# Two-layer encoder with a sorted mixture of experts: rows gathered four blocks ahead, expert matrices in two transfers each

## The reference

```python
def _hier_moe(h, w_group, b_group, w_expert, b_expert, w1, w3, w2):
    pg = jax.nn.softmax((xt @ w_group).astype(jnp.float32) + b_group.astype(jnp.float32), axis=-1)
    g_val, g_idx = lax.top_k(pg, 1)
    ...
    e_val, e_idx = lax.top_k(pe, MOE_TOPK)
    gate = g_val[:, None] * e_val / jnp.sum(e_val, axis=-1, keepdims=True)
    ...
    def expert_block(args):
        xblk, e = args
        return (jax.nn.silu(xblk @ w1[e]) * (xblk @ w3[e])) @ w2[e]

def reference(x, ...):
    for l in range(DEPTH):
        h = _rmsnorm(x, norm_mix[l])
        if l % 2 == 0:
            x = x + _even_mixer(h, ...)
        else:
            x = x + _diff_attention(h, ...)
        h = _rmsnorm(x, norm_ffn[l])
        x = x + _hier_moe(h, ...)
    return _rmsnorm(x, norm_final)
```

## Time and profile before

| | |
|---|---|
| median of 3 runs | 1602.75 us (1597.41 to 1604.11) |
| profiled execution | 1602.87 us, of which the span is 1601.0 us |
| mean granted TensorE clock | 0.931 |
| PE busy, share of the span | 1305.1 us (82%) |
| DVE | 931.1 us (58%) |
| ACT | 504.7 us (32%) |
| POOL | 351.2 us (22%) |
| moved by DMA | 455.63 MB, mean 285 GB/s |
| in 188 transfers of 2048 KB | w1 and w3: 124, median 29.8 us to landing; w2: 64, median 33.2 us |

### The profile page before, as it was taken

How to read it: one execution, slowest core, us unless ns; L and a number is a source line. 1 busy time by engine, 2 the same in 40 slices (tenths; PEclk the granted TensorE clock), 3 DMA queues, 4 the chain that set the end, 5 groups by cost and what they waited for, 6 DMA issues and landing times.

```text
span 1601.0 us, 40258 instructions
## 1 busy us (share of the span) xinstructions
PE 1305.1 (82%) x16222; PEld 850.9 (53%) x16223; DVE 931.1 (58%) x1888; ACT 504.7 (32%) x927; POOL 351.2 (22%) x443
## 2 busy tenths in 40 slices
PE   7998995887887787686999899958858987579884
PEld 5874684554454444355888445845425544346553
DVE  4476635676564556377232896356636765437676
ACT  4416733222221222123223586222212222112222
POOL 4020002333232333132000001023313332213332
PEclk9999996999998899797999999969979999889997
DMA  4313047999999999992232112689999499997972
GB/s 168 106 55 138 2 184 296 406 429 425 429 427 427 428 429 427 428 390 81 102 105 82 49 46 76 252 307 403 429 427 427 168 428 428 425 429 317 426 289 93
DMA packets 60222, 455.63 MB, mean 285 GB/s; under 512 B 6100, under 2 KB 7696, under 8 KB 26816
## 3 DMA queue, kind: packets, MB, share of 16 engines
q1 hardware_dynamic: 53712, 439.01, 66.8%
q0 software_dynamic: 4656, 8.41, 1.4%
q10 hardware_dynamic: 1728, 6.29, 1.0%
HBM read 451.68 MB, written 6.32 MB: 286 GB/s over the span
## 4 chain that ended last, share of the span: by engine, by line
PE 51%; DMA 33%; DVE 7%; issue 5%; ACT 2%; POOL 1%; POOLq 0%; DVEq 0%; SPq 0%; ACTq 0%
DMA wu<-in_w 21%; PE bank L396 18%; DMA xg<-hn_dram,icol 12%; PE bank L856 12%; PE bank L873 4%; PE bank L826 2%; PE bank L816 2%; PE bank L630 2%; PE bank L719 1%; PE bank L731 1%; PE bank L684 1%; DVE hh L1535 1%; PE bank L695 1%; ACT sgate L1123 1%; PE bank L574 1%
## 5 line engine op out<-in xcount | busy, mean ns | idle before, releaser
L856 PE MATMUL bank<-wu,xT 128*32 128x256 f32 x6080 | 388.4, 412 | 137.7 <-DMA wu<-in_w 74.8
L1529 DVE TENSOR_TENSOR X<-bank,X 128x512 f32<-128x512 f32 x776 | 481.0, 682 | 7.5 <-PE bank L826 4.5
L856 PEld LDWEIGHTS bank<-wu,xT 128*32 128x32 f32 x6080 | 212.1, 118 | 286.8 <-issue 192.5
L873 PE MATMUL bank<-wd,hT 128*32 128x256 f32 x3040 | 185.7, 384 | 5.3
L1535 DVE TENSOR_TENSOR hh<-bank,sgate 64x256 f32<-64x256 f32 x95 | 40.4, 426 | 244.2 <-ACT sgate L1123 244.2
L1644 POOL TENSOR_SCALAR Sm<-CT,tgc 128x512 fp32r<-128x512 f32 x95 | 149.4, 1572 | 53.8 <-PE bank L826 53.8
L363 DVE TENSOR_TENSOR wlo<-raw,whi 128x512 fp32r<-128x512 f32 (+1 forms) x112 | 77.1, 699 | 137.5 <-ACT whi L355 137.4
L1123 ACT ACTIVATE sgate<-bank 64x256 f32<-64x256 f32 x95 | 35.8, 377 | 370.9 <-PE bank L856 370.9
L1628 POOL COPY icol<-idxI 128x1 uint32 (+1 forms) x97 | 17.9, 184 | 578.9 <-PE bank L816 552.0
L1130 ACT ACTIVATE yhi<-bank,tgc 128x256 fp32r<-128x256 f32 x95 | 45.0, 474 | 289.1 <-PE bank L826 289.1
L873 PEld LDWEIGHTS bank<-wd,hT 128*32 128x32 f32 x3040 | 101.4, 110 | 63.6 <-issue 25.0
(11 more groups left out here) (227 smaller groups left out, 1656.2 us busy)
## 6 DMA issues: line engine op xcount, KB each, us to landing
wu<-in_w SPq DMA_DIRECT2D x124, 2048.0 KB, 29.8
wd<-in_w SPq DMA_DIRECT2D x64, 2048.0 KB, 33.2
raw<-in_od_w_in SPq DMA_DIRECT2D x12, 1024.0 KB, 5.2
wu<-in_w SPq DMA_DIRECT2D x8, 1024.0 KB, 15.5
raw<-in_ev_w_in SPq DMA_DIRECT2D x6, 1024.0 KB, 5.3
raw<-in_ev_w_out SPq DMA_DIRECT2D x4, 1024.0 KB, 8.1
hn_dram<-HN ACTq DMA_DIRECT2D x8, 512.0 KB, 5.8
raw<-in_od_w_out SPq DMA_DIRECT2D x4, 1024.0 KB, 9.9
```

The costliest lines, as they stand in the source:

```text
L856: last = pe.matmul(B[1][q * SLOT:q * SLOT + SLOT, 0:HH], xT[:, k, :], WU[slot_of(e, q // 2)][:, k, q % 2 * HH:q % 2 * HH + HH], start=k == ...
L873: last = pe.matmul(B[3][q * SLOT:q * SLOT + SLOT, 0:DQ], hT[:, k, :], WD[slot_of(e, 2)][:, k, q * DQ:q * DQ + DQ], start=k == 0, stop=k == ...
L1529: dve.tensor_tensor(xq, B[4 + q][:, :].rearrange("p (t c) -> p t c", t=2), xq, ALU.add).then_inc(signal, 1)
```

## The change

- **Rows.** `xg` has two buffers, for even and odd blocks, each with a semaphore of its own. ACT copies the rows of a block from `xg` to a new tile `xs` at the end of its pass, behind `yhi`, and PE transposes `xs`. The gather of block b+4 follows the selection of block b on POOL, whose loop runs over pairs of blocks. PE does one of the two row transposes ahead of the transposes of `hh` and one behind them. The index tables have NBLK + 4 columns. `Sm` moves to another place in memory.
- **Weights.** Each w1 and w3 comes by two transfers, each of four of the eight k-slices, which are 8 KB per partition; PE's counts are 32, 32 and 16 for the three pieces.
- **End of an expert stage.** The first half of the last token sums goes into banks 0 to 3, the second into banks 4 to 7. PE first waits for the last gathers.
- **Start of layer 0 and of layer 1.** ACT and DVE split the first weight slice of layer 0 ahead of the activations; in both layers the first dense matmuls wait for one `lo` slice at a time.
- **Attention of layer 0.** The exponentials at L1000 move behind the softmax exponentials of the step n = 1, and DVE's multiplies to n = 4 to 7.
- DVE loads `tot` ahead of its wait for `s_vidx`. Several semaphores are put together.

```diff
-        xg = mw.take("xg", [P, DQ])
+        xg = mw.take("xg", [P, 2, DQ])
+        xs = mw.take("xs", [P, DQ])
         xT = mw.take("xT", [P, KD, SLOT])
         hh = mw.take("hh", [2 * SLOT, HH])
         sgate = mw.take("sgate", [P, HH])
         yhi, ylo = mw.take("yhi", [P, DQ], F32R), mw.take("ylo", [P, DQ], F32R)
-        Sm = mw.take("Sm", [P, T], F32R)
-        hT = Region(tail_at + 9 * KB, tail_size - 9 * KB).take("hT", [P, FK, SLOT])
+        tl = Region(tail_at + 8 * KB, tail_size - 8 * KB)
+        Sm = tl.take("Sm", [P, T], F32R)
+        hT = tl.take("hT", [P, FK, SLOT])
...
-                if chunk:
+                if chunk and (k or not first):
                     pe.wait_ge(chunk, base + max(k + 1, first))
                 for a in range(n_banks):
+                    if chunk and first and k == 0:
+                        pe.wait_ge(chunk, base + a + 1)
...
                 if j < 2:
-                    sp.dma_start(WU[k][:, :, :], (w1, w3)[j][l, src].rearrange("e (p k) f -> p (e k) f", p=P)).then_inc(s_piece[k], 16)
+                    for half in range(2):
+                        ks = slice(half * KD // 2, (half + 1) * KD // 2)
+                        sp.dma_start(WU[k][:, ks, :], (w1, w3)[j][l, src].rearrange("e (p k) f -> p (e k) f", p=P)[:, ks, :]).then_inc(s_piece[k], 16)
...
-                def row_transposes():
-
-                    for a in range(2):
-                        last = pe.transpose(B[0][:, a * P:a * P + P], xg[:, a * P:a * P + P], ident)
+                def row_transposes(parts):
+
+                    for a in parts:
+                        last = pe.transpose(B[0][:, a * P:a * P + P], xs[:, a * P:a * P + P], ident)
                     return last
...
+                        token_sums(1)
+                        pe.wait_ge(s_xcp[l], b + 4)
+                        row_transposes((0,))
                         pe.wait_ge(s_tabs, l + 1)
                         pe.wait_ge(s_h[l], b + 1)
                         for a in range(2):
                             last = pe.transpose(B[2][:, 2 * a * SLOT:2 * (a + 1) * SLOT], hh[:, a * P:a * P + P], ident[0:2 * SLOT, 0:2 * SLOT])
                         last.then_inc(s_htr[l], 1)
-                        pe.wait_ge(s_xg[l], 16 * b + 32)
-                        row_transposes().then_inc(s_xtr[l], 1)
+                        row_transposes((1,)).then_inc(s_xtr[l], 1)
...
-                pe.wait_ge(s_xg[l], 16)
-                row_transposes().then_inc(s_xtr[l], 1)
+                pe.wait_ge(s_xcp[l], 3)
+                row_transposes((0, 1)).then_inc(s_xtr[l], 1)
...
-                token_sums(0, {0: (s_add[l], 8 * tot + 1)})
-                token_sums(1, {q: (s_mo[l], q + 1) for q in range(NQ)})
+                pe.wait_ge(s_xT[l], tot + 1)
+                pe.wait_ge(s_xcp[l], tot + 4)
+                for odd in range(2):
+                    pe.wait_ge(s_xg[odd][l], 16 * (tot >> 1) + 32)
+                token_sums(0, bank=0)
+                token_sums(1, bank=0)
+                token_sums(2, {0: (s_add[l], 8 * tot + 1)})
+                token_sums(3)
...
+                splits(0, ks=(0,))
                 mixer_input(0, 0, hi0, range(4))
-                for k in range(4):
+                for k in range(1, 4):
                     splits(0, ks=(k,))
-                    mixer_input(0, 0, hi0, (k + 4,))
+                    mixer_input(0, 0, hi0, (k + 3,))
+                mixer_input(0, 0, hi0, (7,))
...
-                for c in range(4):
-                    act.wait_ge(s_grs, c + 1)
-                    act.activation(hpad[:, c, 0:T], hpad[:, c, 0:T], ACT.Exp, scale=-0.5).then_inc(s_gnr, 1)
...
+                    if n == 1:
+                        for c in range(4):
+                            act.wait_ge(s_grs, c + 1)
+                            act.activation(hpad[:, c, 0:T], hpad[:, c, 0:T], ACT.Exp, scale=-0.5).then_inc(s_gnr, 1)
...
+                for b in range(2):
+                    act.wait_ge(s_xg[b][l], 16)
+                    if b:
+                        act.wait_ge(s_xtr[l], b)
+                    act.activation(xs[:, :], xg[:, b, :], ACT.Copy).then_inc(s_xcp[l], 1)
...
+                    act.wait_ge(s_xg[0][l], 16 * ((b + 2) >> 1) + 16)
+                    act.wait_ge(s_xg[1][l], 16 * ((b + 3) >> 1))
+                    act.wait_ge(s_xtr[l], b + 2)
+                    act.activation(xs[:, :], xg[:, bass.ds(act.snap(b & 1), 1), :].rearrange("p o c -> p (o c)"), ACT.Copy).then_inc(s_xcp[l], 1)
...
-                    if 2 <= n < 6:
-                        c = n - 2
+                    if 4 <= n < 8:
+                        c = n - 4
...
-                add_sums(0, s_mo[l])
+                add_sums(0, s_mo[l], bank=0)
...
-                def gather(b):
+                def gather(b, odd):
 
                     nxt = b + 1 if isinstance(b, int) else pool.snap(b + 1)
-                    pool.wait_ge(s_xtr[l], nxt)
-                    pool.tensor_copy(icol[:, :], idxI[:, b:b + 1] if isinstance(b, int) else idxI[:, bass.ds(b, 1)]).then_inc(s_icol[l], 1)
+                    pool.wait_ge(s_xcp[l], nxt)
+                    pool.tensor_copy(icol[:, odd:odd + 1], idxI[:, b:b + 1] if isinstance(b, int) else idxI[:, bass.ds(b, 1)]).then_inc(s_icol[l], 1)
                     pool.wait_ge(s_hnst, 16 * TT * (l + 1))
                     pool.wait_ge(s_icol[l], nxt)
-                    pool.indirect_dma_start(out=xg[:, :], out_offset=None, in_=hn_dram[l].rearrange("t (q c) -> (t q) c", q=NQ),
-                                            in_offset=bass.IndirectOffsetOnAxis(ap=icol[:, :], axis=0),
-                                            bounds_check=last_row, oob_is_err=False).then_inc(s_xg[l], 16)
+                    pool.indirect_dma_start(out=xg[:, odd, :], out_offset=None, in_=hn_dram[l].rearrange("t (q c) -> (t q) c", q=NQ),
+                                            in_offset=bass.IndirectOffsetOnAxis(ap=icol[:, odd:odd + 1], axis=0),
...
-                gather(0)
-                pool.wait_ge(s_bktfin, 32)
-                pool.tensor_scalar(Sm[:, :], iotaT, neghalf[:, 0:1], None, ALU.is_equal).then_inc(s_sel1[l], 1)
-                gather(1)
+                gather(0, 0)
+                gather(1, 1)
                 pool.wait_ge(s_bktfin, 32)
                 pool.wait_ge(s_gate, 2 * l + 2)
-                with pool.Fori(0, pool.snap(tot - 1)) as b:
-                    gather(pool.snap(b + 2))
-                    selection(b)
-                selection(pool.snap(tot - 1))
+                pool.tensor_scalar(Sm[:, :], iotaT, neghalf[:, 0:1], None, ALU.is_equal).then_inc(s_sel1[l], 1)
+                gather(2, 0)
+                gather(3, 1)
+                pairs = pool.snap(tot >> 1)
+                with pool.Fori(0, pairs) as i:
+                    for odd in range(2):
+                        selection(pool.snap(2 * i + odd))
+                        gather(pool.snap(2 * i + odd + 4), odd)
+                selection(pool.snap(2 * pairs))
```

More of the change, by code:

```diff
@@ L800, in router @@
                     for q in range(NQ):
-                        last = pe.matmul(B[5][q * SLOT:q * SLOT + SLOT, 0:NBLK + 1], slotsel[:, j, :], blkt[:, j, :], start=j == 0, stop=j == 7)
+                        last = pe.matmul(B[5][q * SLOT:q * SLOT + SLOT, 0:NBLK + 4], slotsel[:, j, :], blkt[:, j, :], start=j == 0, stop=j == 7)
                 last.then_inc(s_idx, 1)
@@ L806, in router @@
                     for q in range(NQ):
-                        last = pe.matmul(B[6][q * SLOT:q * SLOT + SLOT, 0:NBLK + 1], slotsel[:, j, :], blkv[:, j, :], start=j == 0, stop=j == 7)
+                        last = pe.matmul(B[6][q * SLOT:q * SLOT + SLOT, 0:NBLK + 4], slotsel[:, j, :], blkv[:, j, :], start=j == 0, stop=j == 7)
                 last.then_inc(s_vidx, 1)
@@ L811, in experts, with token_sums @@
                 pe.wait_ge(s_tabs, l + 1)
-                def row_transposes():
-                    for a in range(2):
-                        last = pe.transpose(B[0][:, a * P:a * P + P], xg[:, a * P:a * P + P], ident)
-                    return last
-                def token_sums(half, waits):
-                    for t in (2 * half, 2 * half + 1):
-                        for part in (yhi, ylo):
-                            for q in range(NQ):
-                                if t % 2 == 0 and part is yhi and q in waits:
-                                    pe.wait_ge(*waits[q])
-                                last = pe.matmul(B[4 + q][:, t % 2 * DQ:t % 2 * DQ + DQ], Sm[q * SLOT:q * SLOT + SLOT, t * P:t * P + P],
-                                                 part[q * SLOT:q * SLOT + SLOT, :], start=part is yhi, stop=part is ylo)
-                    last.then_inc((s_sum, s_sumd)[half][l], 1)
+                def row_transposes(parts):
+                    for a in parts:
+                        last = pe.transpose(B[0][:, a * P:a * P + P], xs[:, a * P:a * P + P], ident)
```

(12 more changed lines are left out.)

115 lines of the change are left out of this document (60 added, 55 removed).

## The result

The changed kernel takes 1587.6 us in the median (1587.14 to 1589.31, 6 runs) beside 1603.05 us of the kernel before in the same runs: a ratio of 0.9906, 95% interval 0.9885 to 0.9926, some 15 us less. Its profiled execution has a span of 1586.8 us (1601.0 before).

A forecast was written before the change was run, and what follows sets the result against it. The weight stream binds three expert stretches, PE two, plus all work ahead of the first experts. From 1602.87 us, -4.8 -1.8 -2.1 -2.2 -2.0 +0.3 = -12.6 gives 1590.3; range 1579 to 1603.

The forecast's parts named there:

- Gather: Expert blocks: gathering four ahead removes PE's waits, gain 4.8 us (4 to 5.7); the other 13 of 18.8 change nothing.
- the bytes are the same: Weight stream: halved w1 and w3 move the same bytes in 124 more transfers, 8 KB runs costing 0 +-0.1 us.
- Halves: Weight stream: two transfers for each w1 and w3 cost 0, between -4 and +18 us (88 x 0.2).
- The rival of an issue's price for each transfer: Weight stream: each of 88 halved matrices pays 0.43 us, 38 in all, giving 1628; chance 0.09.
- the estimate by the fixed cost a transfer: Weight stream: 2 us more for every halved matrix, 176 us for 88, giving 1766; no row shows it.
- Start of layer 0: First dense matmul of layer 0 starts near 15.4 instead of 17.26 us: gain 1.8, between 0 and 3.6.
- more than summed: Rival: shorter PE idle time spares slow-clock time in three places; with a late raw end some 8 us more, 1582; chance 0.11.
- Exponentials: Attention of layer 0: four moved exponentials (2.19 us) fit into a later wait; gain 2.1, between 1 and 2.2.
- Between the layers: End of layer 0: adds back to back, gain 2.2; start of layer 1: dense matmuls released sooner, gain 2.0.
- End of layer 1: Last token sums: PE's wait for the last gather costs 1.7, banks return 1.4 at most: +0.3, between -1 and +1.
- ACT: Each block: row copy costs 0 within 1.85 us of room; rival: 1 us over costs 32, giving 1622, chance 0.05.
- The rival that the early gains do not carry: Whole kernel: early gains are lost in the stream or blocks, leaving about 6 us of gain, 1597; chance 0.20.

The follow-up runs named there:

- a_whole: The changed kernel with w1 and w3 loaded by one transfer each again: 1586.88 us, ratio 0.9903.
- a_best: The changed kernel with whole w1 and w3 transfers and PE's wait for the last gathers behind the first half of the last token sums: 1584.69 us, ratio 0.9885.
- b_early: The kernel before with only the edits outside the blocks; one xg buffer, gathers and weight transfers as before: 1586.61 us, ratio 0.9906.
- b_pstride: The kernel before with w1 and w3 by two transfers each, of even and odd partitions, in 16 KB runs: 1606.1 us, one execution.
- b_split: The kernel before with only the two transfers for each w1 and w3, in 8 KB runs: 1602.62 us, ratio 0.9995.
- a_slack1: The changed kernel with one more ACT copy of 1024 columns in each block, ahead of the gate's table load: span 1589.1 us.
- a_slack2: The changed kernel with two more ACT copies of 1024 columns in each block, ahead of the gate's table load: span 1594.1 us.
- b_phalf: The kernel before with w1 and w3 by two transfers each, of the lower and upper 64 partitions, in 16 KB runs: 2338.2 us, one execution.

## Why the prediction was right, step by step

The time lay 3 us under the forecast of 1590.3, in its range and on its side. Of the steps some were too small, and two parts that I had treated as independent were not. That the total came out so near is in part luck: clock that I had not counted gave some 3 us, and the stream that I had put at nothing took 2.6.

*Gather.* The waits were worth what the PE-bound stretches showed, 4.3 us for the 4.8 taken (a_whole and a_best against before, b_early and b_pstride). That 13 of the 18.8 us would change nothing held too, to about 1 us: the changed kernel was 5.2 us ahead at block 0, 10.2 at block 19, and 4.2 at block 38, behind the full queue, and with whole transfers the gather edit takes the stream from 682.4 to 683.7 us (before, b_early, b_pstride) to 681.4 and 681.7 (a_whole, a_best). The over 12 us from landing to use that I had expected were not there: behind the first four blocks the copy comes some 14 us or more behind the issue, and behind the landing, where the trace has it, 7.4 us at the least. That was room enough. What failed is the step "the bytes are the same" for the halves: it asked what shorter runs do to the piece and not what they do to the other queue that shares the DMA engines. They bring the gather forward, so the halves alone take 3.4 us of the 4.3, and the gather edit beside them 0.9.

*Halves.* Taken as 0 between -4 and +18; the stream pays 2.6 us, 0.03 us for each of 88 matrices. Landings read to 0.1 us, on which the 0 rested, could not show that. The rival of an issue's price for each transfer (38 us) fell with b_split, and so did the estimate by the fixed cost a transfer of the Trainium skill, DMA: Bandwidth & Descriptors, section "Anatomy of one DMA" (176 us): behind a full queue it isn't paid, b_pstride shows no cost beyond some 1 us for twice the transfers. That section fits its 2 us to transfers issued by GpSimd; the weights here are issued by SyncE. Nor did the rule of at least 1 MiB a DMA (the Trainium skill, the same page, section "Rules for kernel authors") speak against this edit, as I had written: the halves have 1 MiB each.

*Start of layer 0.* The first dense matmul starts at 15.49 where 15.4 was expected, 1.8 us earlier:

```profile
15.49 0.47 PE L400 MATMUL bank<-whi,hi 128*128 128x512 f32 x1 [1.31 <-DVE lo L1198]
```

But PE then also ran at full clock, which I had left to the rival "more than summed". The windows of the first 4.5 us of matmuls, before and after:

```profile
17.20:21.70 4.50, 4.44 (x12) 3.49 (x13) 4.45 (x8) 2.69 (x5) 0.00 (x0) 0.62 0.01 5
```

```profile
15.40:20.00 4.60, 4.50 (x20) 3.73 (x21) 4.60 (x8) 4.60 (x10) 0.00 (x0) 1.00 0.29 113
```

Twelve matmuls against twenty: 1.6 us more, 3.4 in all for the 1.8 taken. This one is no chance of one execution: all five kernels here without the edit stood idle for 3.52 us at this place and then ran at 0.50 to 0.62, all nine with it at 1.00 after 0.7 to 1.9 us.

*Exponentials.* The third exponential starts at 140.11 without a wait, 145.90 before:

```profile
140.11 0.69 ACT L1023 ACTIVATE P<-bank,nmx 128x512 f32<-128x512 f32 x1
```

PE's matmuls behind the attention are 4.95 us ahead, those before that place 3.4: 1.6 us for the 2.1 taken.

*Between the layers.* The adds behave as forecast, twelve of them in 7.3 us with no idle time:

```profile
L1558 DVE TENSOR_TENSOR X<-bank,X 128x512 f32<-128x512 f32 x12 | 7.3, 677 | 0.0
```

The sum of 4.2 was too small: kernels with these edits take 341.1 to 342.4 us between the layers, those without 345.5 to 349.0, 6.0 us between the means. From block 44 to the first dense matmul the edit gives 4.5 us of them (29.2 to 24.7 in the mean), near the sum. The rest, 1.5, lies behind that matmul and is the clock again; of the kernels without the edit the 345.5 is b_split, whose dense matmuls found the full clock. So a part of this gain may differ from one execution to the next.

*End of layer 1.* +0.3 forecast, +0.5 measured (32.1 to 31.6, the mean of the kernels without the edit), of two larger terms: the banks give 2.8 us (b_early 28.8) and the wait for a gather that nobody needs takes 3.3. That they nearly cancel was luck, since I had put the banks at 1.4 at most and the wait at 1.7. The instant itself was foreseen: PE starts 3.2 us behind the mask (done at 1564.51), where I had 3.4. What I missed is that without the wait PE would have started much sooner; the row shows 5.0 us of idle time:

```profile
1567.75 0.58 PE L831 MATMUL bank<-yhi,Sm 32*128 32x256 f32 x4 [5.02 <-DMA xg<-hn_dram,icol]
...
1569.02 4.88 DVE L1558 TENSOR_TENSOR X<-bank,X 128x512 f32<-128x512 f32 x8 [2.82 <-PE bank L831]
```

*ACT.* Cost 0, as forecast. The room ahead of the gate fell from 1.85 us by the copy's 0.42:

```profile
346.33 0.38 ACT L1145 ACTIVATE sgate<-bank 64x256 f32<-64x256 f32 x1 [1.45 <-PE bank L862]
```

a_slack1 and a_slack2 put the point from which the rival decides where the idle time says it is.

The rival that the early gains do not carry fell: at the first block of layer 0 the changed kernel is 5.2 us ahead and at its last 5.1 (some 4 forecast), and at the first of layer 1 it is 12.2 ahead (some 8 forecast). In sum, from the means of the table: -6.5 to the first block, -6.0 between the layers, -4.3 for the waits, +2.6 for the stream, +0.5 at the end, -13.7 of the 15 measured. The forecast had its total nearly right with the gather's share about right and that of the clock missing; and it did not see that the change without its two main parts would be as fast.

## What to carry to other kernels

Time a change by its parts as well as in sum: here two edits removed the same wait, a third effect gave the gain back, and the small reorderings at the ends of the stages carried the result. A wait for a small transfer beside a saturated stream can be shortened from the stream's side, by shorter runs, at a price in bandwidth that can be read in GB/s. And idle time of PE ahead of dense work can cost more than its length, when the matmuls behind it start at the lower clock, as they did in five of six traces at one place here and five of five at another.

## What the runs showed of the hardware

- The length of a transfer's runs bears on how long another queue's transfers take beside it: with 16, 8 and 4 KB runs of w1 and w3 (w2 in 8 KB throughout) the gather landed after 6.7, 6.0 and 5.9 us, and the stream ran at 427, 425 and 420 GB/s. The Trainium skill, DMA: Bandwidth & Descriptors, section "Queues, rings and completion order", says that each DMA engine goes round the queues packet by packet and drains a whole packet before it switches; the trace agrees in so far as longer runs hold the gather up. The profile counts one packet for a run; whether the page means the same by a packet no run here shows.
- Two transfers for the lower and the upper 64 partitions ran at a little more than half the rate, with the DMA engines shown as busy all the time; the even and the odd partitions, also 64 for each transfer, ran at 426. The window of the first stream of b_phalf, to be read against that of b_pstride:

```profile
300.00:1030.00 730.00, 368.82 (x4896) 194.30 (x4888) 230.19 (x412) 90.99 (x150) 115.08 (x149) 0.73 1.01 229
```

  The Trainium skill, SBUF — State Buffer, section "Can I just issue two DMAs to hit both halves?", says that two transfers, one at partition 0 and one at partition 64, ran only 6% faster than a single one. The 229 GB/s agree with it. It also says that only one transfer that spans all 128 partitions reaches all 16 ports. The two transfers of b_pstride, each of every second partition, reached the full rate of this stream without that; which ports they used no run shows.
